# Grouping the modulation sections in PSUM, and moving the end of the conv layer norm into the attention loop

## The chip, the cores and the metric

The kernel runs on one core of a Trainium2 chip. The metric is the device time of one execution in microseconds (us), the median of the executions that were timed. Before the change it is 1821.3 us over three runs, from 1820.79 to 1822.1.

## The reference, cut to what matters

Two trunk layers run on 384 tokens (128 context, 256 latent), three tiles of 128. Each layer is a mixer with three parallel groups (a Conformer convolution, a Hyena long convolution, differential attention) and then a mixture of 64 experts. The change touches two pieces of it.

The modulation: one vector for the context tokens and one for the latent ones go through a 1024 x 6144 matrix, and the result is cut into six sections of 1024 (shift, scale and gate of the mixer, and the same for the experts).

```python
mod = cond @ p['w_mod'] + p['b_mod']
sh1, sc1, g1, sh2, sc2, g2 = jnp.split(mod[:, None, :], N_MOD, axis=-1)
h = rms_norm(x, p['g_pre_mix']) * (1.0 + sc1) + sh1
```

The Conformer group, whose layer norm runs over the 256 channels of each token:

```python
a = u[..., :D_CONV] * jax.nn.sigmoid(u[..., D_CONV:])
a = dwconv(a, p['conv_w'], p['conv_b'])
mu = jnp.mean(a, axis=-1); var = jnp.mean(jnp.square(a - mu), axis=-1)
a = (a - mu) * lax.rsqrt(var + EPS) * g + b
return jax.nn.silu(a)
```

## The kernel before, in words

Every engine has its own instruction stream, written out by hand. Semaphores order the streams, and within an engine the order is that of the code.

**Modulation.** The two layers have twelve sections together, and each section comes as two chunks of 2 MB (`wmod`, chunks 0 to 23). `mod_chunk(j)` multiplies one chunk: 16 matmul instructions of 512 columns into PSUM banks 6 and 7, where four groups of 32 rows hold partial sums over the input. When both chunks of a section are in, ScalarE copies the two banks to SBUF (`mod_rows`, line 1278), TensorE multiplies that copy by `FOLD`, which sums the four groups and turns the rows into columns (`mod_columns`, line 612, 16 instructions with 2 moving columns each), and ScalarE copies the 16 columns out (`mod_column`, line 1284). The first two sections (chunks 0 to 3) come at the very start. Chunks 4 to 15 are spread over the attention loop of layer 0, chunks 16 to 23 over that of layer 1, one for each iteration i (`fill`). They alternate between two slots, one in RING and one in KSYS. SyncE issues the load of chunk j + 2 only when TensorE has finished with chunk j (line 388).

**Conv layer norm.** With the channels on partitions, TensorE makes mean and variance with a matmul against a constant (`conv_mean`, line 721). VectorE subtracts the mean, squares, and adds EPS to the variance (line 1877). ScalarE takes the square root (line 1372), VectorE the reciprocal (line 1879), then multiplies both channel halves (line 1881) and applies gain and bias (line 1884). ScalarE takes the sigmoid (line 1375), and VectorE multiplies (line 1887). All of that stands in the streams of VectorE and ScalarE ahead of the attention loop. The result is read by the first `w_out_piece`, in iteration 12 of layer 0 and iteration 9 of layer 1.

**Attention.** Twelve units (three token tiles by four heads) run in a loop of 14 iterations. In iteration i TensorE makes the scores of unit i (line 1100), transposes the probabilities of unit i - 1 (line 1110), does `mod_columns` if one is due, then `mod_chunk`, then probabilities times values of unit i - 1 (line 1130) and the transpose of the output of unit i - 2 (line 1138). VectorE takes the maximum (lines 1918, 1920) and mixes the two maps (lines 1897 to 1904). ScalarE takes the exponentials (line 1389). GpSimd raises one value for each partition to the power -0.5 for each unit (`power`, line 512); this stands for the root of the rms norm, and nothing else is on GpSimd in this stage.

Of the kernel before, what the change touches and what calls it, by code (L numbers as in the profile page):

```python
# [100 lines left out]
def build(nc, I, O):  # L101
    lam_init = [0.8 - 0.6 * math.exp(-0.3 * l) for l in range(DEPTH)]
    with ExitStack() as ctx:
# [16 lines left out]
        COND = sb("COND", [P, KD, MT])  # L120
        FOLD = sb("FOLD", [P, 2])
# [102 lines left out]
        MROWS = (GROW, CO[:, :, :].rearrange("p a b -> p (a b)")[:, 0:2 * DM].rearrange("p (b n) -> p b n", b=2))  # L224
# [77 lines left out]
        def turns(eng, l):  # L302
# [26 lines left out]
            12, 23, 4, 64, 36, 24, 12, 24, 8, 48)  # L329
# [35 lines left out]
        for l_ in range(DEPTH):  # L365
            first_ = [(l_, "h0")] * NT if l_ == 0 else []
            next_ = [(l_ + 1, "h0")] * NT if l_ + 1 < DEPTH else []
            for key_ in first_ + [(l_, "att")] * NUN + [(l_, "y0"), (l_, "h1")] * NT + [(l_, "y1")] * NT + next_:
                n_ += 1
                POW.setdefault(key_, []).append(n_)  # L370
# [134 lines left out]
        def _(pool):  # L505
# [83 lines left out]
            for l in range(DEPTH):  # L589
                for u in range(NUN):  # L590
# [14 lines left out]
        def _(pe):  # L605
            def mod_columns(sec):

                pe.wait_ge(a_mod, 2 * sec + 2)
                if sec > 0:
                    pe.wait_ge(a_col, sec)  # L610
                for k in range(KD):
                    mm = nc.tensor.matmul(PS[5][:, 2 * k:2 * k + 2], MROWS[sec > 1][:, sec % 2, k * P:(k + 1) * P], FOLD[:, :],
# [3 lines left out]
            def mod_chunk(j):  # L616

                a, n = SLOT_OF["m", j]
                part = j % 2
                if j == 0:  # L620
                    pe.wait_ge(d_cond, 3)
                pe.wait_ge(chunk_in[a], 16 * n)
                w = chunk[a].rearrange("p (c n) -> p c n", c=4)
                for hf in (1, 0):
                    for c in range(4):
                        mm = nc.tensor.matmul(PS[6 + hf][MT * c:MT * (c + 1), :], COND[:, 4 * part + c, :],  # L626
                                              w[:, c, hf * 512:(hf + 1) * 512], start=(part == 0), stop=(part == 1))
                    if hf == 1 and part == 1:
# [422 lines left out]
            for l in range(DEPTH):  # L1051

                if l == 0:
# [4 lines left out]
                    mod_columns(0)  # L1058
# [3 lines left out]
                    mod_columns(1)  # L1062
# [30 lines left out]
                for i in range(NUN + 2):  # L1093
# [18 lines left out]
                    j, sec = fill(l, i)  # L1112
                    if sec is not None:
                        mod_columns(sec)
# [50 lines left out]
        def _(act):  # L1165
# [104 lines left out]
            own.sig(sc.activation(COND[:, :, 0:2], cst("cond").rearrange("p (k c) -> p k c", k=KD), ACT.Sigmoid), a_cond)  # L1270
            def mod_rows(sec):

                for hf in (1, 0):
                    if hf == 1:
                        act.wait_ge(mod_half, sec + 1)
                    else:
                        act.wait_ge(mod_used, 2 * sec + 2)
                    sc.activation(MROWS[sec > 1][:, sec % 2, hf * 512:(hf + 1) * 512], PS[6 + hf][:, :], ACT.Copy).then_inc(a_mod, 1)

            def mod_column(sec):  # L1280

                act.wait_ge(pe_mod, sec + 1)
                dst = MODR[:, sec - 6] if sec in (6, 7) else MODC[:, sec % 6]
                sc.activation(dst.rearrange("p k c -> p (k c)"), PS[5][:, 0:2 * KD], ACT.Copy).then_inc(a_col, 1)
# [45 lines left out]
            for l in range(DEPTH):  # L1330
                act.wait_ge(par_in, 16 * (l + 1))
                if l == 0:
                    for t in range(NT):
                        squares(l, 0, t)
                    mod_rows(0)
                    hidden(l, 0)
                    mod_column(0)
                    hidden(l, 1)
                    mod_rows(1)
                    mod_column(1)  # L1340
# [730 lines left out]
```

## Time and profile before

| what | value |
|---|---|
| median of three runs | 1821.3 us |
| the profiled execution: device time, span of its trace | 1823.92 us, 1822.1 us |
| TensorE busy in the span | 1705.8 us (94%) |
| VectorE, ScalarE, GpSimd busy | 617.4, 377.0, 187.2 us |
| share of the DMA queue of the loads | 67.4% of 16 engines |

Times in the rows below are microseconds from the start of the span. PE is TensorE (matmuls), PEld its weight loads, DVE is VectorE, ACT ScalarE, POOL GpSimd, SPq the instruction queue of SyncE. L626 is line 626 of the kernel. The attention loop of layer 0 runs from 204.5 to about 290, that of layer 1 from 1103.0 to about 1178. Between the profile's span and the device time of the same execution lie 1.8 us.

### The profile page before, as it was taken

The numbers are of one execution on the slowest core, as the hardware profiler recorded it, in microseconds if no ns is written. First come the engines' busy times: TensorE is split into PE (matmuls) and PEld (weight loads), VectorE is DVE, ScalarE is ACT, GpSimd is POOL, SyncE is SP. The second block draws the span as 40 slices with busy tenths as digits, with TensorE's granted clock in tenths as the row PEclk, the third lists the DMA queues.
The fourth block names the chain that finished last, engine by engine and source line by source line (L and its number), as shares of the span: only waits on it lengthen the run. The fifth ranks groups of instructions, "written<-read, shape, count | busy, mean of one in ns | idle before, by whom it ended". The sixth has DMA issues, their size and how long they took to land.

```text
span 1822.1 us, 22136 instructions
## 1 busy us (share of the span) xinstructions
PE 1705.8 (94%) x8440; PEld 824.3 (45%) x8440; DVE 617.4 (34%) x1669; ACT 377.0 (21%) x850; POOL 187.2 (10%) x193
## 2 busy tenths in 40 slices
PE   4999799989999999999959997999999999999995
PEld 2555345544444444444435553555444444444442
DVE  1358342422222222222154673433222222222223
ACT  2210343211111111111131014431111111111111
POOL 1000000011111111111110000100111111111110
PEclk9999889999999999999979998998999999999998
DMA  9212581198999999999832137315799999999993
GB/s 398 93 74 93 206 337 69 58 374 338 425 409 418 426 405 422 426 426 426 352 127 93 54 131 263 118 47 213 320 415 425 404 425 412 417 425 426 426 425 135
DMA packets 77147, 541.00 MB, mean 297 GB/s; under 512 B 8304, under 2 KB 11376, under 8 KB 21488
## 3 DMA queue, kind: packets, MB, share of 16 engines
q1 hardware_dynamic: 67248, 503.90, 67.4%
q0 software_dynamic: 9792, 35.66, 4.8%
q8 instruction: 69, 1.13, 0.2%
q14 instruction: 38, 0.31, 0.0%
HBM read 533.76 MB, written 5.77 MB: 296 GB/s over the span
## 4 chain that ended last, share of the span: by engine, by line
PE 87%; DMA 6%; DVE 3%; ACT 2%; issue 1%; SPq 0%; ACTq 0%; POOL 0%; DVEq 0%
PE PSB L836 29%; PE PSB L845 14%; PE PSB L828 7%; PE PSB L823 6%; PE PSB L890 5%; PE PSB L891 5%; PE PSB L791 4%; PE PSB L878 4%; PE PSB L626 2%; DMA RING<-in_wmod 2%; PE PSB L863 1%; DMA X<-in_x 1%; DMA WB<-in_exp_w_up 1%; DMA RING<-in_exp_w_up 1%; DMA KSYS<-in_wmod 1%; PE PSB L852 1%
## 5 line engine op out<-in xcount | busy, mean ns | idle before, releaser
L836 PE MATMUL PSB<-WB,EX 128*32 128x512 f32 (+2 forms) x1408 | 432.1, 598 | 0.2 <-DMA RING<-in_exp_w_up 0.2
L836 PE MATMUL PSB<-RING,EX 128*32 128x512 f32 (+2 forms) x1344 | 417.3, 598 | 3.8 <-DMA WB<-in_exp_w_up 2.1
L845 PE MATMUL PSB<-RING,AT 128*32 128x512 f32 (+2 forms) x720 | 229.8, 602 | 4.9 <-issue 3.8
L1647 DVE TENSOR_TENSOR YL<-PSB,YH 128x512 fp32r<-128x512 f32 x136 | 94.1, 692 | 354.5 <-ACT YH L1246 354.5
L845 PE MATMUL PSB<-WB,AT 128*32 128x512 f32 (+2 forms) x704 | 210.8, 596 | 0.0
L890 PE MATMUL PSB<-YH,SCAT 128*128 128x512 f32 x408 | 172.1, 422 | 2.8 <-DVE YL L1647 2.8
L836 PEld LDWEIGHTS PSB<-WB,EX 128*32 128x32 f32 (+2 forms) x1408 | 113.1, 126 | 136.0 <-issue 136.0
L526 POOL TENSOR_SCALAR SCAT<-CST,LSTT 128x384 fp32r<-128x384 f32 x68 | 85.2, 1252 | 841.6 <-PE PSB L891 841.5
L836 PEld LDWEIGHTS PSB<-RING,EX 128*32 128x32 f32 (+2 forms) x1344 | 105.8, 124 | 124.8 <-issue 124.8
L891 PE MATMUL PSB<-YL,SCAT 128*128 128x512 f32 x408 | 161.2, 395 | 0.0
L1629 DVE COPY EX<-PSB 128x512 f32<-128x512 f32 x68 | 47.0, 692 | 323.4 <-PE PSB L878 323.4
L1246 ACT ACTIVATE YH<-PSB 128x512 fp32r<-128x512 f32 x136 | 81.2, 597 | 239.6 <-PE PSB L845 239.6
L828 PE MATMUL PSB<-RING,HT 128*128 128x512 f32 x288 | 125.6, 592 | 0.0
L823 PE MATMUL PSB<-HT,RING 128*128 128x384 f32 x320 | 109.0, 495 | 3.3 <-ACT HT L1191 3.3
L878 PEld LDWEIGHTS PSB<-CST,XG 128*128 128x128 f32 x544 | 58.8, 141 | 106.9 <-issue 106.9
L845 PEld LDWEIGHTS PSB<-RING,AT 128*32 128x32 f32 (+2 forms) x720 | 63.5, 130 | 79.2 <-issue 79.2
L512 POOL TENSOR_TENSOR ST<-ST,HALF 128x1 f32<-128x1 f32 x48 | 26.4, 550 | 654.1 <-DVE ST L1911 476.6
L845 PEld LDWEIGHTS PSB<-WB,AT 128*32 128x32 f32 (+2 forms) x704 | 58.4, 126 | 72.4 <-issue 71.9
L1239 ACT ACTIVATE SGM<-PSB 128x256 f32<-128x256 f32 x68 | 26.1, 384 | 312.5 <-PE PSB L836 312.5
L878 PE MATMUL PSB<-CST,XG 128*128 128x128 f32 x544 | 88.2, 285 | 0.0
L890 PEld LDWEIGHTS PSB<-YH,SCAT 128*128 128x128 f32 x408 | 77.7, 190 | 21.6 <-issue 4.9
L791 PE MATMUL PSB<-RING,YT 128*128 128x512 f32 x192 | 85.0, 593 | 0.0
(262 smaller groups left out, 1779.0 us busy)
## 6 DMA issues: line engine op xcount, KB each, us to landing
RING<-in_exp_w_gate SPq DMA_DIRECT2D x64, 1024.0 KB, 10.5
RING<-in_exp_w_up SPq DMA_DIRECT2D x64, 1024.0 KB, 13.6
RING<-in_exp_w_down SPq DMA_DIRECT2D x64, 1024.0 KB, 14.1
WB<-in_exp_w_gate SPq DMA_DIRECT2D x64, 1024.0 KB, 11.8
WB<-in_exp_w_up SPq DMA_DIRECT2D x64, 1024.0 KB, 14.4
WB<-in_exp_w_down SPq DMA_DIRECT2D x64, 1024.0 KB, 14.1
RING<-in_wmod SPq DMA_DIRECT2D x14, 2048.0 KB, 10.0
KSYS<-in_wmod SPq DMA_DIRECT2D x10, 2048.0 KB, 9.3
```

The source lines that it names most:

```text
L526: nc.gpsimd.tensor_scalar(SCAT[:, s % 2, :], cst("iota"), LSTT[:, s:s + 1], None, ALU.is_equal).then_inc(p_scat, 1)
L791: mm = nc.tensor.matmul(PS[YB[0][t] + hf][:, :], YT[:, f, t * P:(t + 1) * P], w[:, f, :], start=(f == 0), stop=(f == 7))
L823: mm = nc.tensor.matmul(PS[3 + i % 3][:, 0:TOK], w[:, k, :], HT[:, k, :], start=(k == 0), stop=(k == KD - 1))
L828: mm = nc.tensor.matmul(PS[3 + i % 3][:, :], HT[:, k, t * P:(t + 1) * P], w[:, k, :], start=(k == 0), stop=(k == KD - 1))
L836: mm = nc.tensor.matmul(PS[6][s0:s0 + w, :].rearrange("p (w f) -> p w f", w=2), e[:, k, s0:s0 + w], rawgu[n % NBUF][:, k], start=(k == 0), ...
L845: mm = nc.tensor.matmul(dst[s0:s0 + w, :], AT[:, j, s0:s0 + w], rawdn[n % NBUF][:, hf, j], start=(j == 0), stop=(j == 1))
L878: mm = nc.tensor.transpose(PS[7][:, c * P:(c + 1) * P], XG[:, s % 2, k * P:(k + 1) * P], ident)
L890: nc.tensor.matmul(PS[piece][:, :], w, YHb[s % 2][:, cols], start=False, stop=False, skip_group_check=True)
L891: mm = nc.tensor.matmul(PS[piece][:, :], w, YLb[s % 2][:, cols], start=False, stop=True, skip_group_check=True)
L1246: sc.activation(YHb[s % 2][:, hf * 512:(hf + 1) * 512], PS[6 + hf][:, :], ACT.Copy).then_inc(a_yh, 1)
L1629: v.tensor_copy(EX2[:, s % 2, 4:8, :].rearrange("p k s -> p (k s)"), PS[7][:, :]).then_inc(e_high, 1)
L1647: v.tensor_tensor(YLb[s % 2][:, hf * 512:(hf + 1) * 512], PS[6 + hf][:, :], YHb[s % 2][:, hf * 512:(hf + 1) * 512].bitcast(F32), ALU.subtr ...
```

## The change

`COND` gets six more columns of zeros, and the condition stands in its columns 6 and 7. A section now takes a window of 32 columns of `COND` that starts at 6 - 2 x (its place in its group), so that its two result rows land at two rows of their own in each group of 32, and up to four sections add up in the same PSUM banks before anything is read. There are four groups: sections 0 and 1, 2 to 5, 6 and 7, 8 to 11. `mod_rows`, `mod_columns` and `mod_column` run once for a group, with 4 or 8 moving columns in place of 2. `FOLD` has 8 columns. In layer 0 the columns are made in iterations 8 and 12 (before: 2, 4, 6, 8, 10, 12), in layer 1 in iteration 8 (before: 2, 4, 6, 8). At the start they are made once, after chunk 3.

GpSimd takes the power -0.5 of the whole variance (128 x 384) in one instruction, ahead of its attention work, in place of ScalarE's square root and VectorE's reciprocal. The two multiplications and the gain and bias move into iteration 4 on VectorE. ScalarE takes exp(-x) in iteration 5 in place of the sigmoid, and VectorE makes 1/(1 + e) and the product in iterations 6 and 7, one channel half in each.

```diff
-        COND = sb("COND", [P, KD, MT])
-        FOLD = sb("FOLD", [P, 2])
+        COND = sb("COND", [P, KD, MT + 6])
+        FOLD = sb("FOLD", [P, 8])
...
+        SECS = ((0, 2), (2, 6), (6, 8), (8, 12))
+        GROUP = {s_: g_ for g_, (a_, b_) in enumerate(SECS) for s_ in range(a_, b_)}
...
-            return first + i if i < n else None, (first + i) // 2 - 1 if 0 < i <= n and i % 2 == 0 else None
+            ended = {8: 1, 12: 2} if l == 0 else {8: 3}
+            return first + i if i < n else None, ended.get(i)
...
             for l in range(DEPTH):
+                pool.wait_ge(d_ln, K_LN * l + 5)
+                own.sig(nc.gpsimd.tensor_tensor(SG[:, 0, :], SG[:, 1, :], HALF[:, 0:1].to_broadcast([P, TOK]), ALU.pow), p_pow)
                 for u in range(NUN):
                     power(d_oms, NUN * l + u + 1, 24 + 2 * (u % 2), 1)
...
+                elif sec == first and part == 0:
+                    pe.wait_ge(a_mod, 2 * g)
                 pe.wait_ge(chunk_in[a], 16 * n)
                 w = chunk[a].rearrange("p (c n) -> p c n", c=4)
                 for hf in (1, 0):
                     for c in range(4):
-                        mm = nc.tensor.matmul(PS[6 + hf][MT * c:MT * (c + 1), :], COND[:, 4 * part + c, :],
-                                              w[:, c, hf * 512:(hf + 1) * 512], start=(part == 0), stop=(part == 1))
+                        mm = nc.tensor.matmul(PS[6 + hf][MT * c:MT * (c + 1), :], COND[:, 4 * part + c, at:at + MT],
+                                              w[:, c, hf * 512:(hf + 1) * 512], start=(sec == first and part == 0),
+                                              stop=(sec == last - 1 and part == 1), skip_group_check=True)
...
                     hidden(l, 0)
-                    mod_columns(0)
                     mod_chunk(2)
                     hidden(l, 1)
                     mod_chunk(3)
-                    mod_columns(1)
+                    mod_columns(0)
...
-                act.wait_ge(d_ln, K_LN * l + 5)
-                own.sig(sc.activation(SG[:, 0, :], SG[:, 1, :], ACT.Sqrt), a_ln)
-                act.wait_ge(d_ln, K_LN * l + 10)
-                for c in range(2):
-                    own.sig(sc.activation(SG[:, c, :], CN[:, c, :], ACT.Sigmoid), a_ln)
...
+                    if i == 5:
+                        act.wait_ge(d_ln, K_LN * l + 9)
+                        for c in range(2):
+                            own.sig(sc.activation(SG[:, c, :], CN[:, c, :], ACT.Exp, scale=-1.0), a_ln)
...
-                dve.wait_ge(a_ln, 3 * l + 1)
-                do(v.reciprocal(SG[:, 1, :], SG[:, 0, :]), d_ln)
-                for c in range(2):
-                    sig(v.tensor_tensor(CN[:, c, :], CN[:, c, :], SG[:, 1, :], ALU.mult), d_ln)
...
+                def late_norm(n):
+
+                    if n == 0:
+                        dve.wait_ge(p_pow, POW[l, "cn"][0])
+                        for c in range(2):
+                            sig(v.tensor_tensor(CN[:, c, :], CN[:, c, :], SG[:, 0, :], ALU.mult), d_ln)
+                        own.wait(d_ln)
+                        for c in range(2):
+                            sig(v.tensor_scalar(CN[:, c, :], CN[:, c, :], par("lng")[:, c:c + 1], par("lnb")[:, c:c + 1],
+                                                ALU.mult, ALU.add), d_ln)
+                        return
+                    c = n - 1
+                    dve.wait_ge(a_ln, 2 * (l + 1))
+                    do(v.tensor_scalar(SG[:, c, :], SG[:, c, :], 1.0, None, ALU.add), d_ln)
+                    do(v.reciprocal(SG[:, c, :], SG[:, c, :]), d_ln)
                     sig(v.tensor_tensor(YT[:, c, :], CN[:, c, :], SG[:, c, :], ALU.mult), d_ln)
-                own.wait(d_ln)
...
+                    if i in (4, 6, 7):
+                        late_norm((4, 6, 7).index(i))
```

## Rows read from the trace of the kernel before

**Rows 1.** The page, its first line.
```profile
span 1822.1 us, 22136 instructions
```

**Rows 2.** Chain of waits, start of attention in layer 0: start us, us, what.
```profile
204.43 1.28 ACT L1372
205.73 0.53 ACT SG L1372
206.35 2.56 DVE SG L1879
...
212.35 0.56 DVE YT L1887
...
213.60 0.82 ACT HT L1389 x4
```

**Rows 3.** Timeline of PE, first iterations, both layers: start us, us, instructions [idle before].
```profile
204.94 1.93 PE L626 MATMUL PSB<-RING,COND 128*32 128x512 f32 x16
214.46 0.80 PE L1100 MATMUL PSB<-KT,QT 64*128 64x128 f32 x4 [7.60 <-ACT HT L1389]
...
1112.95 0.80 PE L1100 MATMUL PSB<-KT,QT 64*128 64x128 f32 x4 [7.60 <-ACT HT L1389]
```

**Rows 4.** DMA issues between 204 and 282: KB each, median us to landing.
```profile
KSYS<-in_wmod SPq DMA_DIRECT2D x5, 2048.0 KB, 10.3
```

**Rows 5.** Timeline of SyncE's queue, issues of chunks 6 and 12.
```profile
206.92 0.35 SPq L388 DMA_DIRECT2D RING<-in_wmod  x1
...
248.67 0.33 SPq L388 DMA_DIRECT2D RING<-in_wmod  x1
```

**Rows 6.** Windows of layer 0, then layer 1: ..., PEclk, DMA share, GB/s.
```profile
209.00:214.00 5.00, 0.00 (x0) 0.00 (x0) 3.46 (x8) 2.62 (x6) 0.00 (x0) 0.72 1.04 397
214.00:219.00 5.00, 4.43 (x23) 1.57 (x23) 2.12 (x10) 2.12 (x10) 0.00 (x0) 0.60 0.37 157
...
1110.00:1115.00 5.00, 1.94 (x9) 0.89 (x13) 2.94 (x10) 3.05 (x10) 0.00 (x0) 0.50 0.85 363
```

**Rows 7.** Timeline of PE: chunks 6, 8, 12 and 15, then chunk 23 of layer 1.
```profile
221.50 3.55 PE L626 MATMUL PSB<-RING,COND 128*32 128x512 f32 x16
...
232.98 3.64 PE L626 MATMUL PSB<-RING,COND 128*32 128x512 f32 x16 [1.34 <-DMA RING<-in_wmod]
...
260.10 3.64 PE L626 MATMUL PSB<-RING,COND 128*32 128x512 f32 x16 [2.57 <-DMA RING<-in_wmod]
...
278.08 1.92 PE L626 MATMUL PSB<-KSYS,COND 128*32 128x512 f32 x16 [1.09 <-DMA KSYS<-in_wmod]
...
1149.91 1.92 PE L626 MATMUL PSB<-KSYS,COND 128*32 128x512 f32 x16 [0.70 <-DMA KSYS<-in_wmod]
```

**Rows 8.** Timeline of PE, the folds of section 0 and section 2.
```profile
30.66 3.57 PE L612 MATMUL PSB<-FOLD,GROW 128*128 128x2 f32 x16 [3.28 <-ACT GROW L1278]
...
219.72 1.85 PE L612 MATMUL PSB<-FOLD,CO 128*128 128x2 f32 x16
```

**Rows 9.** Groups by line and form: DVE from 184 to 214, count | busy us, mean ns.
```profile
L1879 DVE RECIPROCAL SG<-SG 128x384 f32<-128x384 f32 x1 | 2.6, 2552 | 12.8 <-ACT SG L1372 12.8
L1881 DVE TENSOR_TENSOR CB<-CB,SG 128x384 f32<-128x384 f32 x2 | 1.0, 556 | 0.0
```

**Rows 10.** Groups by line and form: POOL over the span.
```profile
L526 POOL TENSOR_SCALAR SCAT<-CST,LSTT 128x384 fp32r<-128x384 f32 x68 | 85.2, 1252 | 841.6 <-PE PSB L891 841.5
...
L512 POOL TENSOR_TENSOR ST<-ST,HALF 128x1 f32<-128x1 f32 x48 | 26.4, 550 | 654.1 <-DVE ST L1911 476.6 <-DVE ST L1462 110.3 <-DVE ST L1447 67.2
L578 POOL MEMSET RW<- 128x2322 f32 x2 | 4.1, 2037 | 0.0
L577 POOL MEMSET CB<- 128x858 f32 x2 | 1.6, 814 | 0.1
```

**Rows 11.** Timeline of DVE at 193, and of POOL at 219 with its idle time.
```profile
193.03 0.56 DVE L1877 TENSOR_SCALAR SG<-PSB 128x384 f32<-128x384 f32 x1 [6.00 <-PE PSB L721]
...
219.99 0.55 POOL L512 TENSOR_TENSOR ST<-ST,HALF 128x1 f32<-128x1 f32 x1 [186.55 <-DVE ST L1911]
```

More of the change, by code:

```diff
@@ L605, in _, with mod_columns @@
         def _(pe):
[L606 to L610, printed above, removed]
+            def mod_columns(g):
+                first, last = SECS[g]
+                n = 2 * (last - first)
+                pe.wait_ge(a_mod, 2 * g + 2)
+                if g > 0:
+                    pe.wait_ge(a_col, g)
                 for k in range(KD):
-                    mm = nc.tensor.matmul(PS[5][:, 2 * k:2 * k + 2], MROWS[sec > 1][:, sec % 2, k * P:(k + 1) * P], FOLD[:, :],
+                    mm = nc.tensor.matmul(PS[5][:, n * k:n * (k + 1)], MROWS[g][:, k * P:(k + 1) * P], FOLD[:, 0:n],
                                           start=True, stop=True)
@@ L618, in mod_chunk @@
                 a, n = SLOT_OF["m", j]
-                part = j % 2
+                sec, part = divmod(j, 2)
+                g = GROUP[sec]
+                first, last = SECS[g]
+                at = 6 - 2 * (sec - first)
                 if j == 0:
                     pe.wait_ge(d_cond, 3)
+                elif sec == first and part == 0:
+                    pe.wait_ge(a_mod, 2 * g)
                 pe.wait_ge(chunk_in[a], 16 * n)
@@ L1269, in _, with mod_rows, mod_column @@
             act.wait_ge(d_cond, 1)
-            own.sig(sc.activation(COND[:, :, 0:2], cst("cond").rearrange("p (k c) -> p k c", k=KD), ACT.Sigmoid), a_cond)
-            def mod_rows(sec):
+            own.sig(sc.activation(COND[:, :, 6:8], cst("cond").rearrange("p (k c) -> p k c", k=KD), ACT.Sigmoid), a_cond)
+            def mod_rows(g):
                 for hf in (1, 0):
                     if hf == 1:
-                        act.wait_ge(mod_half, sec + 1)
+                        act.wait_ge(mod_half, g + 1)
                     else:
[L1277 to L1284, printed above, removed]
+                        act.wait_ge(mod_used, 2 * SECS[g][1])
+                    sc.activation(MROWS[g][:, hf * 512:(hf + 1) * 512], PS[6 + hf][:, :], ACT.Copy).then_inc(a_mod, 1)
+            def mod_column(g):
+                act.wait_ge(pe_mod, g + 1)
+                first, last = SECS[g]
+                n = last - first
+                dst = MODR[:, 0:2] if g == 2 else MODC[:, first % 6:first % 6 + n]
+                sc.activation(dst.rearrange("p s k c -> p k s c"),
+                              PS[5][:, 0:2 * KD * n].rearrange("p (k s c) -> p k s c", k=KD, s=n), ACT.Copy).then_inc(a_col, 1)
             def hidden(l, n):
@@ L1391, in _ @@
                                                   accum_out=ST[:, 50 + 2 * (i % 2) + c:51 + 2 * (i % 2) + c]), a_exp)
-                    j, sec = fill(l, i)
-                    if sec is not None:
-                        mod_column(sec)
-                    if j is not None and j % 2 == 1:
-                        mod_rows(j // 2)
+                    j, g = fill(l, i)
+                    if g is not None:
+                        mod_column(g)
+                    if j is not None and j + 1 in (12, 16, 24):
+                        mod_rows(GROUP[j // 2])
                     if 1 <= i <= NUN:
@@ L1675, in _ @@
             dve.wait_ge(const_in, 16)
-            sig(v.tensor_reduce(FOLD[:, :], ident.rearrange("p (j c) -> p c j", c=MT)[:, 0:2, :], AX, ALU.add), d_cond)
+            sig(v.tensor_reduce(FOLD[:, :], ident.rearrange("p (j c) -> p c j", c=MT)[:, 0:8, :], AX, ALU.add), d_cond)
             dve.wait_ge(a_cond, 1)
-            do(v.tensor_tensor(COND[:, :, 0:2], COND[:, :, 0:2], cst("cond").rearrange("p (k c) -> p k c", k=KD), ALU.mult), d_cond)
+            do(v.tensor_tensor(COND[:, :, 6:8], COND[:, :, 6:8], cst("cond").rearrange("p (k c) -> p k c", k=KD), ALU.mult), d_cond)
             def modulation(l, first, last, src):
-                dve.wait_ge(a_col, 6 * l + last)
+                dve.wait_ge(a_col, {(0, 2): 1, (0, 6): 2, (1, 2): 3, (1, 6): 4}[l, last])
                 do(v.tensor_tensor(MODC[:, first:last].rearrange("p s k c -> p (s k) c"),
```

25 lines of the change are left out of this document (9 added, 16 removed).

## The prediction

> **What bounds the kernel now.** I read the page first. The span is 1822.1 us [rows 1], and PE is busy for most of it, so only stretches where PE stands still or does work that goes away can pay. Then I followed the chain of waits around the two places of the change. At the start of attention it runs over ScalarE and VectorE alone: a table load of 1.28 us, the square root, the reciprocal of 2.56 us, the normalisation up to 212.35 + 0.56, and the first exponentials [rows 2]. PE has done the first scores and chunk 4 by 204.94 + 1.93 = 206.87, and then stands for 7.60 us, in both layers [rows 3]. That is the stall which the second part of the change aims at.
>
> Inside attention I read the chunks. Chunk 6 starts at 221.50 and chunk 15 at 278.08 [rows 7], 56.6 us for nine chunks, 6.3 us each. There are two slots, and the load of chunk j + 2 is issued when chunk j has been used. A load takes about 10.3 us to land when another is in flight (one took 260.1 - 248.7 = 11.4) [rows 4, 5, 7], and its use 1.9 to 3.6 us. One turn of a slot is thus 12.2 to 14 us for two chunks, 6.1 to 7 us each. That is as much as the loop needs now: **the loads, not PE's instructions, pace this loop**, and chunks 8, 12 and 15 were waited for [rows 7].
>
> **The moved norm, and the stall.** Without it VectorE takes the first maximum at once, ScalarE needs one table load (1.28 us from 204.43) and the exponentials of 0.82 us [rows 2], so the probabilities are there at about 207, when PE is. The 7.60 us go. What is late next is chunk 6: it was issued at 206.92 [rows 5], behind other loads, and the windows show the DMA engines full until 214 and then a share of 0.37 of five us [rows 6], so it lands at about 216. Before, it was used at 221.50 [rows 7]. Of the 7.60 us only 5.5 arrive at chunk 6. Layer 1 is the same picture: the stall ends at 1112.95 [rows 3], the DMA engines are busy until about 1115 [rows 6], two us later, as in layer 0; I take 5.5 us there too.
>
> **The folds.** Sixteen instructions take 1.85 us, and 3.57 at the start [rows 8]; I take the same for 8 moving columns, since 16 weight loads of 128 x 128 stay (bounds: 1.85 and 2.2). Layer 0 loses four folds of its attention (7.4 us of PE), layer 1 three (5.6 us), with the copies of ScalarE around them. By the pace above most of that lies under the loads. It counts where PE came late to a chunk that had landed. Bounds 0 and 13 us; I take 2 us in layer 0 and 0.5 us in layer 1, near the lower end, because chunks 8, 12, 15 and 23 had waits for their own loads in front of them, two of them right behind a fold [rows 7]. The chunks' matmuls keep their number and shape. The new wait on `a_mod` at the first chunk of a group is met by the fold ahead of it.
>
> **The start.** One fold of 3.57 us at 30.66 goes [rows 8]; behind it PE now waits for chunk 2, whose load was hidden by it, and the remaining fold comes after chunk 3 as before. The wider FOLD and COND cost tenths. I take 0, bounds -2 and +2: the earlier order of PE can bring the last fold 1 us earlier, or find TensorE at its slower level, at which the fold takes 3.57 and not 1.85 us.
>
> **What is added inside attention.** On VectorE: two products and two scalings in iteration 4 (at most 4 x 0.56 = 2.2 us), and in iterations 6 and 7 each an addition, a reciprocal of 2.55 and a product, 0.5 + 2.55 + 0.56 = 3.6 us [rows 9]. Behind them on VectorE stands the mixing of the maps, for which PE's next transposes wait. VectorE is done with maximum and output scaling about 1.5 us into a turn of 6 us, so 3.6 us end at about 5 and the mixing at 6. The cover is the wait for the load; without it each would cost up to 3.6 us. I take 0.5 us for each layer (bounds 0 and 3). On ScalarE: two exponentials of 0.5 us in the table that is loaded already, under the same cover. The reader `w_out_piece` comes two iterations later or more.
>
> **The unknown: the power on GpSimd.** It starts when line 1877 ends, 193.03 + 0.56 [rows 11], on an engine that stood idle for 186.55 us [rows 11]. Behind it in GpSimd's queue stand the small powers of attention. The first was due at 219.99 [rows 11] and will be at about 212; VectorE waits for it, and then PE with the values of unit 1, which stand behind chunk 6, that is at about 218 or 219. So the instruction is free while it takes up to some 25 us. No row shows its duration. From below: a one-operand instruction over 384 elements takes 1.25 us [rows 10]. From above: a power of one element takes 0.550 us, of which the two memsets leave about 0.1 as fixed ((2037 - 814) / (2322 - 858) = 0.835 ns an element, 814 - 858 x 0.835 = 98 ns) [rows 10]; 384 x 0.45 = 174 us if elements don't overlap at all. The ends are a factor of 139 apart, and neither row is near, so I take the geometric middle, sqrt(1.25 x 174) = 15 us, which is 38 ns an element: free, with 10 us to spare. With every factor between the ends equally likely, under 25 us holds ln(25 / 1.25) / ln(139) = 0.61 of it, and over 34 us 0.33.
>
> The Trainium skill, GPSIMD Engine Reference, section 3.1, gives about 2.6 cycles an element for a two-operand add at 1.2 GHz; that would be an estimate of 0.8 us for 384 elements, and no cost here, but it is for an add. The idle row of VectorE, 12.8 us ahead of line 1879, says that the power has VectorE to itself for most of its time [rows 9]. The same page, section 2, says that GpSimd shares its SBUF ports with VectorE, a rule that speaks against putting 384 elements beside VectorE's work; no row shows it.
>
> **The sum.** Layer 0: 5.5 + 2 - 0.5 = 7. Layer 1: 5.5 + 0.5 - 0.5 = 5.5. Start 0. Together 12.5 us. Behind attention the chain is PE work one after another, so what arrives at chunk 15 and chunk 23 arrives at the end. The profiled execution had 1822.1 us of span and 1.8 around it, 1823.9, and would have 1811.4; it stands 2.6 us above the median of 1821.3, and so the forecast is **1808.8 us**. With the power hidden the range of the other terms is a gain of 6 to 20 us (lower: 5 + 5 - 2 - 2; upper: the folds count 7 us more), 1801 to 1815.
>
> **The rivals.**
> First, **the power takes the stall's place**. If it takes T over 25 us, VectorE stands at the first output scaling in iteration 2 and PE soon behind it, in each layer. Meanwhile chunks 7 and 8 land, which gives back some 2.5 us, so each layer costs T - 27.5. The gain of 12.5 is gone at 27.5 + 6.25, about 34 us, 89 ns an element; from there the change is slower. In the middle of what lies above (sqrt(34 x 174) = 77 us) it costs 99 us: 1809 + 99 = 1908 us. At the upper end it is 2100. For it: one element costs 450 ns beyond the fixed part [rows 10]. Against it: that is one element alone, start of a loop and reads included. Chance 0.30.
>
> Second, **the loads take all of it back**. If the earlier chunks only meet a longer queue (chunk 7 is now issued while chunk 6 is in flight, and 11.4 us instead of 10.3 were seen once [rows 5, 7]), nine chunks at up to 0.6 us more give 5 of the 5.5 us back in layer 0 and most of it in layer 1: a gain of 3, 1818 us. For it: the loop is paced by loads already. Against it: a queue that has work all the time should not move less. Chance 0.10, half of it within the bound of what can be told.
>
> Third, **the folds count in full**: PE and not the loads paced the loop. Then up to 13 - 2.5 = 10.5 us more are gained, 1798 us. Against it stand the waits for loads. Chance 0.05.
>
> **How the numbers follow.** The forecast with its own range of 1801 to 1815 has 0.55, the rivals 0.30, 0.10 and 0.05. A measurement of this kernel can tell about 0.2%, 3.6 us, from no change. Faster: 0.55 + 0.05 + 0.05 = 0.65. Within: 0.05 of the second rival and 0.02 of the first, where T lies near 34. Slower: 0.28. For 8 in 10 the range takes in the folds at half and of the first rival T up to about 74 us (1809 + 2 x 46.5 = 1902), which leaves ln(174 / 74) / ln(139) = 0.17 above: 1799 to 1902.
>
> **What would show it.** The first row of all is the 128x384 power on POOL: under 25 us, or over. The stall of 7.60 in front of the second scores should be gone, and a wait for chunk 6 (to about 216) in its place; with the first rival that wait is for POOL by way of VectorE. Chunk 15 should start near 271, chunk 23 near 1137.5. The fold with 8 columns should take 1.85 us. The forecast is wrong first of all if the power has other than tens of ns an element, and then if the turn of a slot changes from 12.5 us.

## The result, and the profile after

The changed kernel takes 1887.66 us (median of 4 runs, 1878.54 to 1894.4) where the kernel before takes 1821.05 us on the same chip: a ratio of 1.0361 [1.0331, 1.0391], slower by 66.6 us where 12.5 us of gain were forecast. The profiled execution went from 1822.1 [rows 1] to 1886.9 us of span, 64.8 us more. It is the first rival: the power on GpSimd lasts 61.53 us and not 15, and in place of the stall of 7.60 us that went, PE now stands for 35 us in each layer.

From the page of the changed kernel: the span, the shares of the chain that ended last by engine, and the power's group (count | busy us, mean ns of one | idle before and its releaser).
```profile
span 1886.9 us, 21851 instructions
...
PE 77%; DMA 10%; POOL 7%; DVE 4%; ACT 1%; issue 1%; SPq 1%; ACTq 0%; DVEq 0%
...
L595 POOL TENSOR_TENSOR SG<-SG,HALF 128x384 f32<-128x384 f32 x2 | 123.1, 61534 | 308.1 <-DVE SG L1889 308.1
```
In the page of the kernel before the chain had PE 87%, DMA 6% and POOL 0%. Two things are new in it, then: 7% of the span on GpSimd, which is the two powers (123.1 of 1886.9), and 4 points more of DMA, which nobody had priced.

How the power gets into the chain is read from the chain of waits of the changed kernel in layer 0 (start us, us, what):
```profile
190.15 61.53 POOL SG L595
251.68 0.53 POOL ST L516
252.30 0.36 DVE RW L1945
252.67 0.14 issue
252.80 0.77 PE PSB L1143 x2
```
L516 is the small power of unit 0, one element and half a microsecond of work, which stood behind the wide one in GpSimd's queue. VectorE waited for it with the first output scaling (L1945), and PE with the values of unit 1 (L1143). The same on VectorE, from its timeline (idle before in brackets), with the two reciprocals of iterations 6 and 7:
```profile
252.30 0.35 DVE L1945 TENSOR_SCALAR RW<-PSB,ST 128x128 f32<-128x128 f32 x1 [44.42 <-POOL ST L516]
...
273.62 2.55 DVE L1904 RECIPROCAL SG<-SG 128x384 f32<-128x384 f32 x1
...
280.09 2.55 DVE L1904 RECIPROCAL SG<-SG 128x384 f32<-128x384 f32 x1
```
And PE's timeline of the changed kernel, the places of [rows 3, 7, 8]:
```profile
203.27 0.49 PE L1113 MATMUL PSB<-KT,QT 64*128 64x128 f32 x4
...
214.05 3.64 PE L639 MATMUL PSB<-RING,COND 128*32 128x512 f32 x16 [6.75 <-DMA RING<-in_wmod]
252.80 0.77 PE L1143 MATMUL PSB<-QKV,HT 128*128 128x128 f32 x2 [35.11 <-DVE RW L1945]
...
277.80 0.55 PE L1123 MATMUL PSB<-CST,HT 128*128 128x128 f32 x3 [1.90 <-DVE HT L1919]
...
284.27 0.55 PE L1123 MATMUL PSB<-CST,HT 128*128 128x128 f32 x3 [2.25 <-DVE HT L1919]
284.66 1.85 PE L620 MATMUL PSB<-FOLD,CO 128*128 128x8 f32 x16
...
303.58 1.93 PE L639 MATMUL PSB<-KSYS,COND 128*32 128x512 f32 x16 [0.78 <-DMA KSYS<-in_wmod]
...
1147.54 3.64 PE L639 MATMUL PSB<-RING,COND 128*32 128x512 f32 x16 [7.01 <-DMA RING<-in_wmod]
1186.03 0.77 PE L1143 MATMUL PSB<-QKV,HT 128*128 128x128 f32 x2 [34.84 <-DVE RW L1945]
```
Line by line: the second scores (203.27) have no wait, so the 7.60 us of [rows 3] did go. Chunk 6 is waited for instead, until 214.05. Behind it PE stands for 35.11 us, and for 34.84 in layer 1. The new VectorE work makes the transposes of two iterations late by 1.90 and 2.25 us. The fold of eight columns takes the 1.85 us of the fold of two [rows 8], at a granted clock of 0.98. Chunk 15 starts at 303.58 where it started at 278.08 [rows 7], and the forecast wanted 271. The stand has a second effect: TensorE's granted clock is 0.50 by its end (230 to 250), the lower of its two levels, and chunk 7 behind it takes 3.64 us (254.85, clock 0.50) where in the kernel narrow below, without the stand, it takes 1.93 (clock 1.00).

To see where the 64.8 us arose I cut each profile at the same instructions: the first tile of the mixer's input projection at PE (u), the first scores, PE's first gate product behind the attention loop, the first copy into EX (the input of the experts' matmuls), the first square of the norm behind the mixture and the end. The stretches between them, in us, for all kernels of this study (each from one profiled execution; attention is first scores to first gate product, mixture is first copy into EX to the square, or to the end in layer 1):

| kernel | u tile starts | attention 0 | mixture 0 | attention 1 | mixture 1 | span |
|---|---|---|---|---|---|---|
| before | 50.1 | 86.2 | 528.8 | 74.6 | 546.4 | 1822.1 |
| changed | 46.6 | 115.2 | 533.2 | 107.3 | 550.6 | 1886.9 |
| norm_only | 50.1 | 117.3 | 528.7 | 110.0 | 547.2 | 1880.5 |
| fold_only | 47.8 | 84.3 | 533.2 | 73.8 | 550.5 | 1820.6 |
| narrow | 47.4 | 81.3 | 531.9 | 70.6 | 549.5 | 1821.0 |
| tanh | 47.9 | 78.2 | 531.8 | 68.5 | 548.8 | 1809.7 |
| shift | 50.0 | 81.9 | 532.9 | 76.3 | 550.5 | 1824.4 |
| fold_pad | 46.8 | 86.8 | 530.8 | 73.4 | 547.8 | 1816.3 |
| tanh_pad | 46.8 | 79.5 | 530.8 | 70.7 | 547.5 | 1805.9 |
| tanh_ring | 46.6 | 76.5 | 530.5 | 71.3 | 545.5 | 1800.8 |
| power128 | 47.3 | 81.8 | 529.5 | 70.8 | 547.6 | 1810.9 |
| power256 | 47.8 | 91.8 | 530.6 | 83.7 | 550.2 | 1840.5 |
| after_pad | 48.2 | 114.0 | 530.6 | 110.5 | 546.6 | 1879.6 |

Attention has +29.0 and +32.7, the start -3.5, the mixtures +4.4 and +4.2, the rest (between these stretches) -2.0. Attention is nearly all of it, but 8.6 us lie in the mixtures, where not one instruction was changed. A single stretch is not exact: attention 0 has the same instructions in before (86.2) and shift (81.9), and again the same ones in fold_only (84.3) and fold_pad (86.8). The granted clock goes with it: over that stretch it is 0.84 in before and 0.88 in shift, 0.88 in fold_only and 0.84 in fold_pad, so part of the scatter is TensorE at its lower level for longer or shorter. Also, the routing stretches between attention and mixture jump between 98.1 and 102.6 in layer 0 and 92.0 and 98.1 in layer 1 from one kernel to the next. The mixtures fall into groups within 2 us, with one exception. So I use means over kernels that share a stretch where there are several, and differences of one or two us between two single stretches are no findings.

### The profile page after: what moved, and what is told of

Read it like the earlier page. It is cut to its first block, busy times and chain, and to the rows that moved or that the text cites. A ratio compares the mean times of both kernels' runs of the same rounds, so it can differ in the third digit from the quotient of the medians.

```text
span 1886.9 us, 21851 instructions
## 1 busy us (share of the span) xinstructions
PE 1691.7 (90%) x8312; PEld 808.4 (43%) x8312; DVE 623.6 (33%) x1675; ACT 361.1 (19%) x820; POOL 310.2 (16%) x195
## 4 chain that ended last, share of the span: by engine, by line
PE 77%; DMA 10%; POOL 7%; DVE 4%; ACT 1%; issue 1%; SPq 1%; ACTq 0%; DVEq 0%
PE PSB L850 26%; PE PSB L859 12%; POOL SG L595 7%; PE PSB L842 6%; PE PSB L837 6%; PE PSB L904 4%; PE PSB L905 4%; PE PSB L805 4%; PE PSB L892 4%; DMA WB<-in_exp_w_up 4%; DMA RING<-in_exp_w_up 4%; DMA RING<-in_wmod 2%; PE PSB L639 1%; PE PSB L877 1%; DMA KSYS<-in_wmod 1%
## 5 line engine op out<-in xcount | busy, mean ns | idle before, releaser
L595 POOL TENSOR_TENSOR SG<-SG,HALF 128x384 f32<-128x384 f32 x2 | 123.1, 61534 | 308.1 <-DVE SG L1889 308.1
L523 POOL DMA_INDIRECT XG<-h_rows,IDX x68 | 70.0, 1029 | 125.4 <-DVE LSTW L1611 97.3
## 6 DMA issues: line engine op xcount, KB each, us to landing
RING<-in_exp_w_down SPq DMA_DIRECT2D x64, 1024.0 KB, 14.5
WB<-in_exp_w_gate SPq DMA_DIRECT2D x64, 1024.0 KB, 12.2
```

What stands on the lines that cost most here:

```text
L595: own.sig(nc.gpsimd.tensor_tensor(SG[:, 0, :], SG[:, 1, :], HALF[:, 0:1].to_broadcast([P, TOK]), ALU.pow), p_pow)
```

## Experiments

### One part at a time

**fold_only** is the changed kernel with its old norm; **norm_only** is the kernel before with only the norm moved. Their edits are the two halves of the diff above.

> Only the grouping of the modulation sections; the conv layer norm stays ahead of attention as before, with its stall of 7.6 us in each layer. Theory A (the wide power on GpSimd is the whole loss, the rest of the change gains): the start gains the 3.5 us that the changed kernel showed, the folds some 3 us more, 1821 - 6.5 = 1814.5 us. Rival (the folds lay under the loads altogether and their grouping delays something): 1817 us or more. Rival (folds were on PE's path in full): 1821 - 3.5 - 13 = 1804.5 us. The stretch from the first scores to the first w_out after the loop, 88 us before, should be 85 by A.

> Only the moved conv layer norm with the 128x384 power on GpSimd; folds and start as before. Theory A: the power takes 61.5 us again, PE waits about 35 us for the first scaled output in both layers, and the time is above that of the changed kernel by what the grouping gains, 1888 + 6.5 = 1894 us. Rival (the grouping has a part in the loss): under 1885 us.

Measured: fold_only 1821.28 us against 1821.38, ratio 0.9996 [0.9981, 1.0011]; norm_only 1886.33 us, ratio 1.0360 [1.0335, 1.0385]. The whole loss is the norm's. Both missed the number expected of them, 1814.5 and 1894 us, by 7 us, and for one reason: the 6.5 us that the grouping was to gain do not come out. On POOL and then PE of norm_only (two timelines):
```profile
193.68 61.53 POOL L591 TENSOR_TENSOR SG<-SG,HALF 128x384 f32<-128x384 f32 x1 [160.55 <-DVE SG L1877]
255.19 0.54 POOL L512 TENSOR_TENSOR ST<-ST,HALF 128x1 f32<-128x1 f32 x1
```
```profile
217.71 3.64 PE L628 MATMUL PSB<-RING,COND 128*32 128x512 f32 x16 [5.19 <-DMA RING<-in_wmod]
256.33 0.77 PE L1132 MATMUL PSB<-QKV,HT 128*128 128x128 f32 x2 [34.98 <-DVE RW L1933]
```
The power has the same 61.53 us and PE the same wait, now with the old sections. fold_only gains nothing, though it starts 2.3 us earlier: its two mixtures are each 4 us longer, as in the changed kernel. norm_only has them at 528.7 and 547.2. So what lengthens a mixture came with the sections.

### The same move with a power that is small

The variance is the same number in all 128 partitions, so the wide power computes each of 384 values 128 times. **narrow** takes the variance as three columns (six matmuls of one column), powers 128 x 3 elements, and has three matmuls with the identity spread the result over the partitions again:

```diff
-                own.sig(nc.gpsimd.tensor_tensor(SG[:, 0, :], SG[:, 1, :], HALF[:, 0:1].to_broadcast([P, TOK]), ALU.pow), p_pow)
+                own.sig(nc.gpsimd.tensor_tensor(ST[:, 60:63], ST[:, 9:12], HALF[:, 0:3], ALU.pow), p_pow)
...
+                            mm = nc.tensor.matmul(PS[2][:, t:t + 1], SG[:, c, t * P:(t + 1) * P], cst("mean")[:, 0:1],
+                                                  start=(c == 0), stop=(c == 1))
...
+            def spread(l):
+                pe.wait_ge(p_pow, POW[l, "cn"][0])
+                for t in range(NT):
+                    mm = nc.tensor.matmul(PS[2][:, t * P:(t + 1) * P], ST[:, 60 + t:61 + t].to_broadcast([P, P]), ident,
+                                          start=True, stop=True)
...
+                late_norm(0)
                 for i in range(NUN + 2):
...
-                    if i in (4, 6, 7):
-                        late_norm((4, 6, 7).index(i))
+                    if i in (6, 7):
+                        late_norm(i - 5)
```

> The changed kernel, with the variance made as one column for each of the three token tiles, the power taken of 128x3 elements (estimate 0.55 + 2 x 0.16 = 0.87 us at the 160 ns an element of the wide one), and the result spread over the partitions by three small matmuls; the two products and the gain and bias stand ahead of attention, in VectorE's idle time. Theory A: no wait for GpSimd; start -3.5, stall -5.5 in each layer, folds -3, reciprocals in iterations 6 and 7 +2 in each layer: 1821 - 3.5 - 11 - 3 + 4 = 1807.5 us. Rival (loads take the gain back, and the mixture runs slower behind it as it did in the changed kernel, by 5 us): 1815 us or more.

Measured: 1816.09 us, ratio 0.9968 [0.9953, 0.9984], against 0.9996 for fold_only. The move itself gains; the power was what made it a loss. But 1807.5 us were expected, and the rival with longer mixtures had 1815 or more. Attention is 33.9 and 36.7 us shorter than in the changed kernel. Yet against fold_only it is shorter by 3.0 and 3.2 us only, where the stall alone was to give 5.5. The timeline of PE in narrow shows where the rest is:
```profile
251.76 0.90 PE L1138 MATMUL PSB<-CST,HT 128*128 128x128 f32 x3 [2.13 <-DVE HT L1935]
```
It is the transpose behind VectorE's reciprocal, as in the changed kernel at 277.80 and 284.27. **tanh** takes the reciprocal out, by sigmoid(x) = 0.5 tanh(x / 2) + 0.5:

```diff
-                            own.sig(sc.activation(SG[:, c, :], CN[:, c, :], ACT.Exp, scale=-1.0), a_ln)
+                            own.sig(sc.activation(SG[:, c, :], CN[:, c, :], ACT.Tanh, scale=0.5), a_ln)
...
-                    do(v.tensor_scalar(SG[:, c, :], SG[:, c, :], 1.0, None, ALU.add), d_ln)
-                    do(v.reciprocal(SG[:, c, :], SG[:, c, :]), d_ln)
+                    do(v.tensor_scalar(SG[:, c, :], SG[:, c, :], 0.5, 0.5, ALU.mult, ALU.add), d_ln)
```

> As narrow, but the sigmoid is 0.5 + 0.5 tanh(x/2), so that iterations 6 and 7 have no reciprocal of 2.55 us on VectorE. Theory A: the waits of 1.9 and 2.2 us that PE had behind them go, 4 us less than narrow, 1803.5 us, if tanh needs no table load of its own. Rival (these waits only ran alongside the waits for loads): the same time as narrow. If tanh has its own table, two loads of 1.28 us for each layer come under cover or cost up to 5 us.

Measured: 1811.23 us, ratio 0.9945 [0.9926, 0.9964]; attention shorter again by 3.1 and 2.1 us. Over the three kernels that have the tanh and no added power, the two attention stretches together are 148.2 us in the mean (146.7 to 150.2) against 151.9 in narrow: the reciprocals, 2 x 5.1 us of VectorE, cost 3.7 us on the path. In layer 0 tanh_pad has narrow's granted clock (0.87) and is 1.8 us shorter, so it isn't the clock alone. The medians of narrow and tanh differ by 4.9 us, with intervals that overlap from 0.9953 to 0.9964, so the stretches carry this more than the times do. ScalarE's timeline (here of tanh_pad, the same kernel with a pad, below) has the two tanh between exponentials and no table load beside them:
```profile
231.10 0.49 ACT L1406 ACTIVATE HT<-PSB 128x384 f32<-128x384 f32 x1 [0.81 <-PE PSB L1139]
231.49 0.92 ACT L1410 ACTIVATE SG<-CB 128x384 f32<-128x384 f32 x2
232.31 0.57 ACT L1417 ACTIVATE HT<-PSB,ST 128x384 f32<-128x384 f32 x1
```
0.92 us for both is less than one load of 1.28 [rows 2]. The Trainium skill, ScalarE: Activation LUTs, section "Table sets", lists tanh in the set of exp; the trace agrees.

### What lengthens the mixtures

The sections make COND and FOLD wider, by 192 bytes in each partition, and every tile declared behind them starts 192 bytes later. Modulo 512 bytes, WB (one of the two destinations of the expert weights) moves from 0 to 192, XG from 0 to 192, KSYS from 96 to 288; RING, declared earlier, stays at 128. **shift** is the kernel before with nothing but an unused tile of 192 bytes there. **fold_pad** is fold_only with 320 unused bytes, which bring all three back to their old places modulo 512; **tanh_pad** is tanh with the same.

```diff
+        sb("pad", [P, 48])
```
(48 floats in shift, 80 in fold_pad and tanh_pad; behind the declaration of FOLD.)

> The kernel before with one unused tile of 192 bytes a partition behind FOLD, so that every tile behind it lies where the changed kernel has it (WB, XG and the attention tiles at 192 and not at 0 past a multiple of 512 bytes). Nothing else. Theory C (the grouping's loss is that shift: loads into shifted tiles run slower, and the mixture is paced by its loads): the two mixtures 532 to 533 and 550 us instead of 528.8 and 546.4, together 1821 + 8 = 1829 us. Rival D (it is the order of the work, or chance, and addresses do nothing): 1821 us with mixtures of 528.8 and 546.4.

> fold_only with an unused tile of 320 bytes behind FOLD, which puts every later tile back to its old place modulo 512 bytes. Theory C: mixtures 528.8 and 546.5 again, so 1821 - 8 = 1813 us: the start's 2.3 to 3.5 us and some 3 us of the folds come out at the end. Rival D: 1821 us as fold_only.

> tanh with the same 320 bytes. Theory C: 1811 - 6 = 1805 us (mixtures 528.8 and 546.5 instead of 531.8 and 548.8). Rival D: 1811 us.

Measured, against before at 1821.03 us: shift 1826.4, ratio 1.0025 [1.0013, 1.0037]; fold_pad 1815.62, 0.9966 [0.9950, 0.9981]; tanh_pad 1806.93, 0.9916 [0.9901, 0.9931]. An unused tile alone costs 5.4 us. Its mixtures are 532.9 and 550.5 us, the changed kernel's to within 0.4, and together 8.1 us longer than those of before; the interval of the times allows 2.4 to 6.7 us, so the stretches of single profiles may overstate it. All kernels of the study fall into three groups: 528.7 and 546.8 us in the mean for the two with the old places (before, norm_only); 532.6 and 550.0 for the five that are shifted; 530.5 and 547.9 for the five with the 320 bytes. Mixture 1 of power256, 550.2, is the exception (547.4 without it). By these stretches the shift costs 3.8 and 3.1 us, and the pad gives some 2 of each back. By the times the pad gives 0.30% to fold_only (0.9996 to 0.9966) and 0.29% to tanh (0.9945 to 0.9916), as much as the shift takes (0.25%). Whether it gives everything back stays open. The chain by engine, from the pages of shift, of fold_only and of fold_pad, against PE 87% and DMA 6% before:
```profile
PE 80%; DMA 12%; DVE 4%; ACT 2%; issue 1%; SPq 1%; ACTq 0%; POOL 0%; DVEq 0%
```
```profile
PE 80%; DMA 12%; DVE 3%; ACT 2%; issue 1%; SPq 1%; ACTq 0%; POOL 0%; DVEq 0%
```
```profile
PE 84%; DMA 9%; DVE 4%; ACT 2%; issue 1%; SPq 0%; ACTq 0%; POOL 0%; DVEq 0%
```
The same order is in the DMA issues of the expert weights (KB each, median us to landing), shift and then fold_pad:
```profile
RING<-in_exp_w_gate SPq DMA_DIRECT2D x64, 1024.0 KB, 11.4
RING<-in_exp_w_up SPq DMA_DIRECT2D x64, 1024.0 KB, 14.7
...
WB<-in_exp_w_gate SPq DMA_DIRECT2D x64, 1024.0 KB, 12.4
```
```profile
RING<-in_exp_w_gate SPq DMA_DIRECT2D x64, 1024.0 KB, 10.2
RING<-in_exp_w_up SPq DMA_DIRECT2D x64, 1024.0 KB, 13.9
...
WB<-in_exp_w_gate SPq DMA_DIRECT2D x64, 1024.0 KB, 11.4
```
And PE's waits in the first mixture (in total, times, longest us) of shift; in the kernel before the same two are 0.6 and 0.2 us in all:
```profile
PE PSB L837 <- DMA WB<-in_exp_w_up: 1.8, 3, 0.8
...
PE PSB L837 <- DMA RING<-in_exp_w_up: 1.0, 2, 0.5
```
The windows of the first mixture, before and then shift (us, busy time and instructions of the engines, PEclk, DMA share, GB/s):
```profile
391.60:920.40 528.80, 522.65 (x2899) 230.75 (x2899) 132.72 (x359) 86.45 (x169) 74.24 (x65) 1.00 0.96 400
```
```profile
387.30:920.10 532.80, 524.62 (x2899) 231.47 (x2899) 132.73 (x359) 86.46 (x169) 74.17 (x65) 1.00 0.97 398
```
The same 2899 matmuls at the same granted clock of 1.00, and DMA engines that are busy nearly all the time in both, in shift for a larger share (0.97). That GB/s are fewer over a longer stretch says nothing by itself, so here is a window of equal length inside it, of before, shift and fold_pad:
```profile
450.00:850.00 400.00, 400.00 (x2289) 174.95 (x2282) 102.43 (x282) 66.57 (x130) 58.15 (x52) 1.00 1.00 420
```
```profile
450.00:850.00 400.00, 399.00 (x2272) 174.77 (x2266) 101.75 (x281) 65.79 (x129) 57.78 (x51) 1.00 1.01 418
```
```profile
450.00:850.00 400.00, 400.00 (x2278) 175.09 (x2272) 101.76 (x281) 66.27 (x130) 58.82 (x52) 1.00 1.00 420
```
The loads move 0.5% less in shift (418 for 420 GB/s), and with the pad they are back at the old rate. 0.5% of 529 us is 2.6 us. In PE's own account the 4 us are 2.0 of standing (528.8 - 522.65 = 6.15 us before, 532.8 - 524.62 = 8.18 in shift) and 2.0 of longer busy time for the same matmuls. In fold_pad (530.8 us, busy 524.13) the standing is nearly back, 6.67 us, and the busy time is not; why it isn't, no run here shows.

That the start of a tile makes the difference is shown; which tile's, and how, is not. Loads into RING, which did not move, land later too, but they share the DMA engines with those into WB. The Trainium skill, DMA: Bandwidth & Descriptors, section "How a descriptor splits into AXI transactions", says that a read which does not start at a multiple of 256 bytes fetches from the boundary below and costs extra beats. It speaks of reads and not of the side that writes into SBUF. If it held there too, WB at 192 would be dearer than at 0, as seen, and RING at 128 should have been dear all along. **tanh_ring** tries the latter: RING too at a multiple of 512, WB and XG as in tanh_pad.

```diff
+        sb("pad", [P, 96])
...
-        sb("pad", [P, 80])
+        sb("pad2", [P, 48])
...
-        MODR = sb("MODR", [P, 6, KD, 2])
+        MODR = sb("MODR", [P, 2, KD, 2])
```

> tanh_pad with RING moved by 384 bytes too, so that RING and WB both start at a multiple of 512 bytes (in every kernel so far RING lies 128 past one). If what counts in theory C is the distance from a multiple of 512 for every load, the mixtures get shorter by up to 4 us each than in tanh_pad, 1797 us; if RING's 128 costs nothing (a multiple of 128 may do), 1805 us; by rival D 1811 us.

Measured: 1809.09 us, ratio 0.9933 [0.9917, 0.9950], not to be told from tanh_pad's 0.9916. Its first mixture, 530.5, is tanh_pad's; its second, 545.5, is 2.0 us shorter. RING's place costs nothing that this measurement finds, so the runs fit that reading of the rule for WB at most, and not for RING.

### The price of a power, and what hides it

The prediction had given the wide power a rule: free up to 25 us, then T - 27.5 for each layer. **power128** and **power256** test it on the best kernel: tanh_pad with a further power right behind the narrow one, whose result nobody reads, over 128 and over 256 elements.

```diff
+                nc.gpsimd.tensor_tensor(RWF[:, 0:128], cst("mean")[:, 0:1].to_broadcast([P, 128]), HALF[:, 0:1].to_broadcast([P, 128]), ALU.pow)
```

> tanh_pad with one more instruction on GpSimd behind the narrow power and ahead of attention's small powers: a power of 128x128 into a part of RW that nobody reads. At 160 ns an element 20.9 us, from 190.8 to about 212. Theory A (only what lasts past PE's wait for chunk 6 at about 218 costs): the same time as tanh_pad, 1807 us, although the first small power, before at 208, comes 4 us late. Rival (any delay of GpSimd's small powers is paid in full): 8 us more, 1815 us.

> The same with 128x256, 41.3 us, from 190.8 to about 232. Theory A with the rule of the forecast (T - 27.5, T being 42.2 with the narrow power ahead of it): 15 us in each layer, 1807 + 29 = 1836 us, and PE waits about 16 us for the first scaled output in layer 0. Rival (paid in full from 208 on): 24 us in each layer, 1855 us.

Measured, against before at 1818.89 us on another chip (so I compare ratios): power128 1808.3, ratio 0.9942 [0.9925, 0.9958]; power256 1836.8, ratio 1.0099 [1.0082, 1.0116]. POOL's timeline of power128 and of power256:
```profile
190.45 0.86 POOL L596 TENSOR_TENSOR ST<-ST,HALF 128x3 f32<-128x3 f32 x1 [157.84 <-DVE ST L1906]
191.28 20.73 POOL L597 TENSOR_TENSOR RW<-CST,HALF 128x128 f32<-128x128 f32 x1
211.98 0.55 POOL L517 TENSOR_TENSOR ST<-ST,HALF 128x1 f32<-128x1 f32 x1
```
```profile
191.72 41.13 POOL L597 TENSOR_TENSOR RW<-CST,HALF 128x256 f32<-128x256 f32 x1
232.83 0.55 POOL L517 TENSOR_TENSOR ST<-ST,HALF 128x1 f32<-128x1 f32 x1
```
and PE's, power128 and then power256:
```profile
214.88 3.64 PE L641 MATMUL PSB<-RING,COND 128*32 128x512 f32 x16 [6.36 <-DMA RING<-in_wmod]
218.46 0.80 PE L1160 MATMUL PSB<-QKV,HT 128*128 128x128 f32 x2
```
```profile
215.68 3.64 PE L641 MATMUL PSB<-RING,COND 128*32 128x512 f32 x16 [6.72 <-DMA RING<-in_wmod]
...
233.98 0.77 PE L1160 MATMUL PSB<-QKV,HT 128*128 128x128 f32 x2 [14.65 <-DVE RW L1962]
```
With 20.73 us the small power is done at 212.5, before chunk 6 has even landed, and the values of unit 1 (L1160) follow chunk 6 with no wait. With 41.13 us they are waited for 14.65. With the narrow power of 0.86 us ahead of it, T is 42.0, and the rule gives 42.0 - 27.5 = 14.5 for each layer (as expected, 15); the attention stretches are 12.2 and 13.0 us longer than tanh_pad's. The whole kernel loses more: the ratios differ by 1.83%, 33 us or 16.7 for each layer, where the rule gives 29. In the two profiles 25 of the 34.5 us lie in attention, and the rest in stretches without a changed instruction, among them 4.5 in the routing and 2.7 in mixture 1. So the rule is right to a few us; the rival, with 24 us for each layer, is out. For 20.73 it gives nothing, and the stretches are 2.3 and 0.1 longer; the two ratios are 0.26% apart (4.7 us) with intervals that overlap a little, so whether it is wholly free stays open by a few us. The time goes with the size: 0.55 us for 1 element in each partition, 0.86 for 3, 20.73 for 128, 41.13 for 256, 61.53 for 384. That is about 0.4 us and 0.16 us for each element, all the way.

**after_pad** is the changed kernel with the 320 bytes of the pad.

> The changed kernel with the unused tile of 320 bytes behind FOLD, so that all later tiles lie as in the kernel before modulo 512 bytes. Theory C: 5 to 6 us under the changed kernel, 1888 - 5.5 = 1882 us, with mixtures of 528.8 to 531 and 546.5 to 548. Rival (the shift matters only where the loads are the bound and hides behind the wait for the power): 1888 us.

Measured: 1880.6 us, ratio 1.0352 [1.0326, 1.0377] where the changed kernel has 1.0361 [1.0331, 1.0391]. The times don't tell the two apart. In the profiles the mixtures are 2.6 and 4.0 us shorter; a second attention stretch that is 3.2 us longer and a later start take most of it back. So for the changed kernel itself the share of the tiles' places rests on the stretches and on shift, not on this ratio.

## Why the prediction was wrong

Each term of the sum over both layers in us (minus is a gain). Attention is the two stretches together, in means: 159.5 for before and shift, 159.2 for fold_only and fold_pad, 148.2 for the three with tanh, 151.9 for narrow, 223.5 for the changed kernel and after_pad. The kernels of one mean lie within 3.6 us.

| term | predicted | measured | from |
|---|---|---|---|
| the stall goes | -11.0 | -11.0 | attention, tanh less fold_only |
| folds in attention | -2.5 | -0.3 | attention, fold_only less before |
| new VectorE work | +1.0 | +3.7 | attention, narrow less tanh |
| the power | 0 | +71.6 | attention, changed less narrow |
| the start | 0 | -3.5 | first u tile, changed less before |
| mixtures | 0 | +8.6 | mixtures, changed less before |
| the rest | 0 | -4.3 | stretches between -2.0, and -2.3 by which the changed kernel's own attention lies off its mean and before's off its |
| sum | -12.5 | +64.8 | |

The row of the power is what is left between two kernels. It also has in it the two products and two scalings of iteration 4, which narrow makes ahead of attention, and the lower clock behind the stand.

**The power** is the step that failed. I bounded it by 1.25 and 174 us and took the geometric middle, 15 us, which is 38 ns an element; it is 160. Its mechanism was right in the first rival: 61.5 - 27.5 = 34.0 for each layer, against 33.9 and 36.7 (changed less narrow, layer by layer); and the waits of 35.11 and 34.84 at the named place. The closeness is partly luck: that PE is at its lower clock behind the stand (chunk 7 in 3.64 us for 1.93) was in no term. What was wrong was to treat the two ends as equally far. The lower one was another operation (a comparison with a scalar), the upper one was the same operation on the same engine, [rows 10], and missed only by its fixed part: I read 0.1 us off memsets, and 0.4 us is what the sizes 1 and 3 give ((0.858 - 0.550) / 2 = 0.154 us an element, 0.55 - 0.15 = 0.4). With 0.4 as fixed part the 174 us would have been 384 x 0.15 = 58 us, and the rival the forecast.

**The stall** was right in total, 5.5 for each layer, and so was what comes late next: chunk 6 is waited for until 214.05 (forecast: about 216), and that is the load, 6.75 us of wait. Where the gain arrives was not right. Counted from the first scores, chunk 6 starts at 15.7 and 16.5 us in fold_only and at 12.4 and 11.8 in tanh (layers 0 and 1), so 3.3 and 4.7 us are there at chunk 6, and the forecast had the whole 5.5 there. The exact 11.0 is in part luck, from stretches that scatter by 3 us.

**The folds** take 1.85 us each whether 2 or 8 columns move, as taken, but only at the higher clock: in narrow the fold of eight columns at 252.46 takes 3.42 us at a granted clock of 0.50, which the bounds of 1.85 and 2.2 left out. 13 us less of them on PE shorten attention by nothing that can be told. The waits say where they went: in the two attention stretches PE waits for loads of chunks 10.5 us before and 20.4 in fold_only. So 9.9 of the 13 us came back as waits, and the loads pace the loop even more strictly than the 2.5 us had it. So the second and the third rival are out: the kernels with tanh keep the stall's gain in full, and the folds don't count in full.

**The new VectorE work** was mis-sized: 0.5 for each layer was taken and 1.9 came for iterations 6 and 7 alone (the work of iteration 4 isn't measured apart), inside the bounds of 0 and 3. The cover that I named, the wait for the load, is not there in each of the two iterations: where the chunk had landed (278.28 in the changed kernel, no wait before it) the 1.90 us of the late transpose have no wait for a load to hide in.

**The start** was wrong by 3.5 us, outside its bounds of 2; over the ten kernels with the new sections it gains 1.9 to 3.5. I had said that PE would wait for chunk 2 in place of the fold. The timeline of the changed kernel:
```profile
30.61 3.51 PE L639 MATMUL PSB<-RING,COND 128*32 128x512 f32 x16 [3.47 <-DMA RING<-in_wmod]
...
38.54 1.95 PE L620 MATMUL PSB<-FOLD,GROW 128*128 128x4 f32 x16 [1.10 <-ACT GROW L1291]
...
46.56 13.78 PE L837 MATMUL PSB<-HT,RING 128*128 128x384 f32 x42 [1.69 <-ACT HT L1204]
```
The chunk starts at 30.61, which is when the fold started before, 30.66 [rows 8]: it had landed by then. I had asked what the fold hid, and not looked when that load had landed. So in the changed kernel nearly the whole fold of 3.57 is gained.

**The mixtures** were in no term. The text looked at what the wider FOLD and COND cost to compute (tenths) and not at where the tiles behind them come to lie.

The range held the time, thanks to the rival; the direction that it called likelier was the wrong one.

## What to carry to other kernels

Price an instruction from a row of the same operation on the same engine, with its fixed part and its slope from two sizes of it, and don't average it with another operation's price; where the same value stands in every partition, compute it once and spread it (61.5 us became 0.86). A long instruction costs nearly nothing until the next one in its queue is due, and about one to one from there: name that next instruction and its due time. When a tile grows, look at where the tiles behind it land; a pad costs nothing to try, and tanh_pad with one is the fastest kernel clearly found here, 0.9916 [0.9901, 0.9931] of the time before (tanh_ring is level with it).

## What the runs showed of the hardware

- A power on GpSimd takes 0.16 us for each element of a partition, with 0.4 us fixed, from 1 to 384 elements (0.55, 0.86, 20.73, 41.13 and 61.53 us); a comparison with a scalar on the same engine takes 1.25 us for 384 [rows 10], a factor of 49 less.
- 192 bytes of an unused tile cost 5.4 us of 1821 (ratio 1.0025 [1.0013, 1.0037]), and 3 to 4 us in each mixture of some 530 us whose loads keep the DMA engines at a share of 0.96; in an equal window the loads move 418 in place of 420 GB/s, and a pad of 320 bytes brings 420 back. How it comes about is open.
- Sixteen matmuls with weights of 128 x 128 take 1.85 us with 2 or 8 moving columns at a granted clock of 0.96 and 0.98, and 3.42 us with 8 at 0.50. After TensorE had stood for 35 us, the granted clock was 0.50, and a chunk took 3.64 us that takes 1.93 at 1.00.
- What a long GpSimd instruction does to wide VectorE work beside it was not seen: VectorE stood idle for 44.42 of the 61.53 us.
